# Input projection: late modulation blocks beside the first units, and twenty units as ten pairs of seven half-size products

## The chip, the cores and the metric

The kernel runs on one core of one Trainium2 chip. The metric is device time in microseconds (us) from start to end of one execution. The core has a matrix engine (TensorE, "PE" in rows), a vector engine (VectorE, "DVE"), a scalar engine (ScalarE, "ACT"), GpSimd ("POOL") and SyncE ("SP"), which here only issues DMAs. Each engine works through its own instructions in order and waits on semaphores that the others raise.

## The reference

One layer of a decoder trunk over T = 1088 tokens (1024 of a prompt, 64 of samples). What matters here is its first half:

```
mod = silu(c) @ w_ada + b_ada                    # c: 9 rows, w_ada: 1024 x 6144
h = rmsnorm(x, g_mix) * (1 + sc1) + sh1          # 1088 x 1024
z = h @ w_in                                     # columns: u, q, k, v, o, ig, fg, gp, gm
d = window means of u - u                        # pooling mixer
q, k, v, ig, fg -> mLSTM in chunks of 128 tokens
```

Everything is float32.

## The kernel before

**A split matmul.** TensorE multiplies rounded fp32r operands. For float32 accuracy each operand is split: ScalarE copies it rounded ("hi"), VectorE subtracts that from the original ("lo"), and TensorE sums three products, hi x hi, hi x lo and lo x hi. The activations h lie split in `act_hi` and `act_lo` (128 partitions, 8 blocks of 128 inputs each, 1088 tokens).

**A unit** is 128 output columns of a weight matrix over all 1088 tokens: its 512 KB of weights are loaded into `raw` (two slots), split into `w_hi` and `w_lo` by `split_hi` (L1028) and `split_lo` (L1588), and multiplied in 8 blocks x 3 products x 3 column groups (384, 384, 320) = 72 matmuls of L2340 into three PSUM banks of `dense` (two sets, turn by turn). `evac` (L1124, L1126) copies the sums to `stage`, and a DMA stores them in the DRAM scratch `z`.

**The input projection's first part** (`l1_part`) is 28 units after the gate unit, in z's order: u (4 units), q, k, v (8 each). The first runs together with the gate unit, so 27 stand in the stretch that changes. The mLSTM's second part (`U_L2` on) needs q, k and v back from z: `qk_load` and `v_load` wait until the stores have landed.

**Late modulation blocks.** 14 blocks of 256 columns of `w_ada` aren't needed until the second part. One goes with every two units: SyncE loads 1 MB into `ada_w`, ScalarE and VectorE split it (`wa_hi`, `wa_lo`), TensorE multiplies it with `c_hl` (16 matmuls, L2460 and L2461), ScalarE copies the result to `ada_rows`, TensorE turns it (L2471), and VectorE adds it to `mod` (L1706, L1709).

**Gate tables.** From ig and fg come small tables for the mLSTM; they are written to DRAM and read back in other layouts by SyncE (L605 to L621), in its one queue with all weight loads. TensorE turns the tables and the pooling history `hrow` (L2526) after the unit at which they are due. GpSimd computes the pooling mixer (L936 to L948), behind the history.

**The feed-forward part** has the scheme that the change brings to the input projection: seven products of half-size blocks in place of eight (Winograd's form of Strassen's scheme), with weight sums on VectorE (L2058 to L2065), splits of 512 columns (L1334, L2047), products of 24 matmuls of 272 columns (L2760), and partial sums taken by ScalarE (L1382 to L1394) and added by VectorE (L2100 to L2112). It runs two such chains side by side, turn by turn.

## Time and profile before

| | |
|---|---|
| median of 3 runs (lowest to highest) | 1964.58 us (1964.14 to 1965.5) |
| the profiled execution's own time | 1967.0 us |
| its span, first to last instruction | 1965.3 us |
| mean granted TensorE clock | 0.989 of full speed |
| busy: PE, DVE, ACT, POOL | 1908.4, 829.4, 621.2, 128.4 us |

The profile is of one execution. "Busy" counts an engine's own instructions, not its waits. In rows of a timeline the bracket at the end is the idle time just before, and what ended it; a row of the timeline that ends in x3 or x16 is several equal instructions in a row.

### The profile page before, as it was taken

How to read it: one execution, taken by the hardware profiler on the slowest of the kernel's cores; microseconds unless marked ns; L12 is line 12 of the kernel's file. 1: busy time of each engine (PE TensorE's matmuls, PEld its weight loads, DVE VectorE, ACT ScalarE, POOL GpSimd, SP SyncE). 2: the span in 40 equal slices, each digit the busy share in tenths (PEclk: the TensorE clock that was granted, in tenths of full speed). 3: DMA queues.
4: the chain of work that ended last, by engine and by line, in shares of the span. 5: the costliest groups of instructions: out<-in, count | busy, mean ns of one | idle time of the engine just before them, and what ended most of it. 6: DMA issues, size and time to landing. Idle time of an engine off the chain costs nothing.

```text
span 1965.3 us, 30471 instructions
## 1 busy us (share of the span) xinstructions
PE 1908.4 (97%) x12193; PEld 1815.0 (92%) x12193; DVE 829.4 (42%) x1363; ACT 621.2 (32%) x952; POOL 128.4 (7%) x245
## 2 busy tenths in 40 slices
PE   7999999999999999999999997899999999999998
PEld 4799989999999997777899997899999999999998
DVE  5422222213334333232553558844455545564542
ACT  4331222222434433121210215533333334343432
POOL 0010009201000002221000000000000000000000
PEclk9999999999999999999999998999999999999999
DMA  8653434452343345544642350422232223774641
GB/s 273 239 177 120 132 122 135 140 151 73 93 128 106 92 150 129 165 142 143 203 123 89 90 175 25 109 67 67 71 111 80 65 65 119 261 240 149 214 152 63
DMA packets 254045, 257.70 MB, mean 131 GB/s; under 512 B 15476, under 2 KB 213160, under 8 KB 253952
## 3 DMA queue, kind: packets, MB, share of 16 engines
q1 hardware_dynamic: 244830, 222.81, 37.7%
q10 hardware_dynamic: 7721, 29.25, 3.7%
q0 software_dynamic: 1408, 4.46, 0.8%
q8 instruction: 58, 0.95, 0.2%
q14 instruction: 28, 0.22, 0.0%
HBM read 189.97 MB, written 66.63 MB: 131 GB/s over the span
## 4 chain that ended last, share of the span: by engine, by line
PE 92%; DVE 3%; ACT 2%; DMA 1%; issue 1%; SPq 0%; ACTq 0%; DVEq 0%
PE dense L2340 44%; PE dense L2760 17%; PE dense L2805 10%; PE misc L2760 5%; PE misc L2805 3%; PE misc L2641 2%; PE misc L2628 1%; PE misc L2567 1%; PE misc L2571 1%; PE misc L2540 1%; DMA ada_w<-in_w_ada_dram 1%; PE dense L2414 1%; PE misc L2569 1%; PE misc L2461 1%; PE misc L2460 1%
## 5 line engine op out<-in xcount | busy, mean ns | idle before, releaser
L2340 PE MATMUL dense<-act_hi,w_hi 128*128 128x384 f32 x1704 | 401.2, 343 | 5.8 <-DVE act_lo L1593 3.0
L2340 PE MATMUL dense<-act_lo,w_hi 128*128 128x384 f32 x1704 | 377.4, 329 | 0.0
L2340 PE MATMUL dense<-act_hi,w_lo 128*128 128x384 f32 x1704 | 376.9, 329 | 0.0
L2340 PEld LDWEIGHTS dense<-act_hi,w_hi 128*128 128x128 f32 x1704 | 291.9, 189 | 28.3 <-issue 21.4
L2340 PEld LDWEIGHTS dense<-act_hi,w_lo 128*128 128x128 f32 x1704 | 293.0, 189 | 0.0
L2340 PEld LDWEIGHTS dense<-act_lo,w_hi 128*128 128x128 f32 x1704 | 292.0, 189 | 0.0
L1588 DVE TENSOR_TENSOR w_lo<-raw,w_hi 128x1024 fp32r<-128x1024 f32 x73 | 92.4, 1267 | 265.9 <-ACT w_hi L1028 265.8
L1124 ACT ACTIVATE stage<-dense 128x768 f32<-128x768 f32 x52 | 42.2, 812 | 285.1 <-PE dense L2340 285.0
L1028 ACT ACTIVATE w_hi<-raw 128x1024 fp32r<-128x1024 f32 x73 | 77.3, 1060 | 167.7 <-PE dense L2340 167.3
L2047 DVE TENSOR_TENSOR w_lo<-hmT,w_hi 128x512 fp32r<-128x512 f32 x120 | 78.9, 686 | 101.2 <-ACT w_hi L1334 101.2
L1334 ACT ACTIVATE w_hi<-hmT 128x512 fp32r<-128x512 f32 x120 | 72.6, 623 | 81.2 <-PE dense L2760 80.8
L2760 PE MATMUL dense<-act_hi,w_hi 128*128 128x272 f32 x528 | 89.0, 291 | 7.0 <-DVE sums L2100 5.6
L2760 PE MATMUL dense<-first_ops,w_hi 128*128 128x272 f32 x528 | 89.1, 291 | 4.2 <-DVE first_ops L2074 4.2
L2760 PE MATMUL dense<-act_lo,w_hi 128*128 128x272 f32 x528 | 87.7, 288 | 1.8 <-DVE w_lo L2047 1.8
L2760 PEld LDWEIGHTS dense<-act_hi,w_hi 128*128 128x128 f32 x528 | 75.7, 191 | 7.9 <-issue 7.0
L2760 PEld LDWEIGHTS dense<-first_ops,w_hi 128*128 128x128 f32 x528 | 75.4, 191 | 4.7 <-DVE first_ops L2074 2.8
L2760 PEld LDWEIGHTS dense<-act_lo,w_hi 128*128 128x128 f32 x528 | 74.7, 188 | 2.2 <-DVE w_lo L2047 2.2
L2228 DVE TENSOR_TENSOR w_lo<-raw,w_hi 128x1024 fp32r<-128x1024 f32 x34 | 41.6, 1224 | 60.1 <-ACT w_hi L1472 60.0
L2228 DVE TENSOR_TENSOR wx_lo<-stage,wx_hi 128x1024 fp32r<-128x1024 f32 x32 | 39.1, 1225 | 58.1 <-ACT wx_hi L1472 58.0
L2760 PE MATMUL dense<-last_op,w_hi 128*128 128x272 f32 x352 | 59.4, 292 | 2.9 <-issue 2.9
L1472 ACT ACTIVATE w_hi<-raw 128x1024 fp32r<-128x1024 f32 x34 | 36.0, 1059 | 75.2 <-PE misc L2805 37.0
L1472 ACT ACTIVATE wx_hi<-stage 128x1024 fp32r<-128x1024 f32 x32 | 33.8, 1059 | 71.5 <-PE misc L2805 40.2
(435 smaller groups left out, 3051.2 us busy)
## 6 DMA issues: line engine op xcount, KB each, us to landing
z_scratch<-stage ACTq DMA_DIRECT2D x52, 544.0 KB, 2.7
raw<-in_w_in_dram SPq DMA_DIRECT2D x53, 512.0 KB, 3.8
ada_w<-in_w_ada_dram SPq DMA_DIRECT2D x24, 1024.0 KB, 5.5
hmT<-in_w_gate_up_dram SPq DMA_DIRECT2D x40, 512.0 KB, 6.1
raw<-in_w_down_dram SPq DMA_DIRECT2D x34, 512.0 KB, 4.4
stage<-in_w_down_dram SPq DMA_DIRECT2D x32, 512.0 KB, 4.4
stage<-z_scratch SPq DMA_DIRECT2D x24, 544.0 KB, 3.7
a_scratch<-sums SPq DMA_DIRECT2D x34, 272.0 KB, 4.8
```

Of the source, the lines that this page charges most:

```text
L1028: act.activation(w_hi[:, n % 2, :], raw[:, n % 2, :], ACT.Copy).then_inc(hi_ready, 1)
L1124: act.activation(wide(stage[:, k % 2, :]), tile_wide(k), func)
L1334: act.activation(w_ops(d, st, q)[0], w_src(d, st, q), ACT.Copy).then_inc(whi_ready, 1)
L1472: act.activation(down_ops(v)[0], down_raw(v), ACT.Copy).then_inc(downhi_ready, 1)
L1588: dve.tensor_tensor(w_lo[:, n % 2, :], raw[:, n % 2, :], w_hi[:, n % 2, :].bitcast(F32), ALU.subtract).then_inc(raw_free[n % 2], 1)
L2047: dve.tensor_tensor(lo, w_src(d, st, q), hi.bitcast(F32), ALU.subtract).then_inc(wlo_ready, 1)
L2228: dve.tensor_tensor(lo, down_raw(v), hi.bitcast(F32), ALU.subtract).then_inc(downlo_ready, 1)
L2340: ins = pe.matmul(tile(k, c), w[:, n % 2, off:off + P], x[:, xr, t0:t1], start=(first and p == 0), stop=(last and p == 2))
L2414: ins = pe.matmul(ada_bank(e), cT[:, kk, :], w[:, kk, :], start=(kk == 0), stop=(kk == KT - 1))
L2641: give(pe.matmul(bank(r, E1), kb[:, b, P * a:P * a + P], vs[:, :], start=True, stop=True), r)
L2760: ins = pe.matmul(out[:, c, :], w[:, P * kt:P * kt + P], x[:, kt, HB * c:HB * c + HB], start=(st in FRESH and kt == 0 and p == 0), stop=(k ...
L2805: ins = pe.matmul(down_bank(ph, o, n), w[p // 2][:, 512 * f + P * o:512 * f + P * o + P], a[p % 2][:, f, 0:n], start=(u == 0 and f == 0 an ...
```

## The change

`l1_part` is gone. Units 1 to 7 after the gate unit's partner run one by one, each with two late modulation blocks between its eight blocks of inputs (`between`): half a block's product after input blocks 1 and 2, its turn after 4; the next one's halves after 5 and 6, its turn after 7. Splits of modulation blocks are done in halves too, and `ada_w` has two slots. The other 20 units become ten pairs: 256 columns over 1088 tokens as seven products of a half-size weight block (512 inputs x 128 columns) and a half-size activation block (512 inputs x 544 tokens). Four sums of activation blocks are made once, by GpSimd from `act_hi` and `act_lo` (ten operations of 2176 columns into `t32`), and split by `t_high` and `t_low`. The pooling mixer on GpSimd starts after all late modulation blocks. Pairs split their weights into halves of slot 0 of `w_hi` and `w_lo`; odd pairs are loaded into slot 1's place (`raw_a`, `raw_b`), even ones into `raw`.

```diff
-U_L1, U_L2, U_GM, U_BP, U_BM, U_OUT, U_FFN = 1, 29, 45, 53, 57, 65, 73
-T_SS, T_GATE, T_L1, T_L2, T_YP, T_BP, T_BM, T_OUT = 0, 1, 2, 30, 54, 58, 66, 74
+U_L1, U_L2, U_GM, U_BP, U_BM, U_OUT, U_FFN = 1, 9, 25, 33, 37, 45, 53
+T_SS, T_GATE, T_L1, T_L2, T_YP, T_BP, T_BM, T_OUT = 0, 1, 2, 10, 34, 38, 46, 54
...
+PAIRS, PAIR_ROW, PAIR_LOOPS = 10, 8, 4
+W0, WS0, G0, GU0 = STEPS * PAIRS, 4 * PAIRS, PAIRS, 16 * PAIRS
...
+        T_OPS = ((t12[:, 0], t12[:, 1]), (t12[:, 2], t12[:, 3]), (t34[:, 0], t34[:, 2]), (t34[:, 1], t34[:, 3]))
+        IN_OPS = (act_block(0, 0), act_block(1, 0), T_OPS[1], T_OPS[0], T_OPS[2], act_block(1, 1), T_OPS[3])
...
+            a, b = pair_raw(p)
+            return (a[:, 0:KB], a[:, KB:2 * KB], a[:, 0:KB], s1b, b[:, 0:KB], a[:, KB:2 * KB], b[:, KB:2 * KB])[st]
...
+            slot, r = (1, st) if p == 0 and st < 2 else (0, (STEPS * p + st) % 2)
+            return w_hi[:, slot, KB * r:KB * r + KB], w_lo[:, slot, KB * r:KB * r + KB]
...
+        def pair_banks(p, st):
+            if st % 2 == 0:
+                return bank_pair(0 if p % 2 == 0 else 3)
+            return bank_pair(1 if st == 1 else 2)
...
+            def late_ada_load(b):
+                if b >= 2:
+                    sp.wait_ge(ada_cut, 2 * (b - 1))
...
+            def pair_load(p, i=0):
+                for u in range(2):
+                    src = w_cols(w_in[0], i * (4 * P) + P * (PAIR_ROW + 2 * p + u))
+                    if u == 0:
+                        if p == 0:
+                            sp.wait_ge(raw_free[1], 4)
+                            sp.wait_ge(raw_free[0], 5)
+                        elif p == 1:
+                            sp.wait_ge(p_done, 2)
+                        else:
+                            sp.wait_ge(wlo_ready, at(p, STEPS, -STEPS, i))
+                    sp.dma_start(pair_raw(p)[u].rearrange("p (k n) -> p k n", k=KT), src).then_inc(gu_in[p % 2], 16)
+            load(4, w_cols(w_in[0], 3 * P))
+            for j in range(1, 5):
+                late_ada_load(2 * j)
+                load(j + 4, w_cols(w_in[0], P * (j + 3)))
+                late_ada_load(2 * j + 1)
+            for b in (10, 11):
+                late_ada_load(b)
...
-            l1_loads(4, 6)
-            load(28, w_cols(w_in[0], 27 * P))
+            for b in (12, 13):
+                late_ada_load(b)
+            pair_load(0)
+            pair_load(1)
+            with sp.Fori(0, PAIR_LOOPS) as i:
+                pair_load(2, i)
+                pair_load(3, i)
...
+            sp.wait_ge(wlo_ready, STEPS * (PAIRS - 1))
+            for j in range(2):
+                l2_load(j)
+            halves_out(6)
+            sp.wait_ge(p_done, STEPS * (PAIRS - 1) + 4)
             for c in range(2):
                 qk_load(c, c)
...
+            t1, t2_, t3, t4 = (t32[:, n] for n in range(4))
+            t_sum(t1, half_of(act_hi, 0, 1), half_of(act_hi, 0, 0))
+            t_sum(t2_, half_of(act_lo, 0, 1), half_of(act_lo, 0, 0))
+            t_done(t1, t1, t2_, ALU.add)
...
+            pool.wait_ge(ada_cut, 2 * ADA_LATE)
+            wait_full(pool, round_full, R_HROW)
...
+            def ada_high(b, half):
+                wait_full(act, ada_in, b, inc=16)
+                if b and half:
+                    wait_full(act, round_full, R_LATE["prod", b - 1])
+                elif b:
+                    act.wait_ge(half_prod, EP0 + b)
+                k0 = KH * half
+                act.activation(wa_hi[:, k0:k0 + KH, :], ada_w[:, b % 2, k0:k0 + KH, :], ACT.Copy).then_inc(adahi_ready, 1)
...
+            def prod_high(p, st, i=0):
+                if st == 0:
+                    act.wait_ge(gu_in[p % 2], i * 32 + 32 * (p // 2 + 1))
+                if st in (2, 3, 4, 5):
+                    act.wait_ge(wsum_ready, at(p, 4, {2: 3, 3: 1, 4: 2, 5: 4}[st], i))
+                if p or st > 3:
+                    act.wait_ge(p_done, at(p, STEPS, st - 1, i))
+                elif st < 2:
+                    wait_full(act, tile_full, T_L1 + 6)
+                else:
+                    wait_full(act, tile_full, T_L1 + 7)
+                act.activation(pair_ops(p, st)[0], pair_src(p, st), ACT.Copy).then_inc(whi_ready, 1)
...
+            def pair_take(p, st, n, sem_, i=0):
+                u, h = ((0, 0), (0, 1), (1, 1), (1, 0))[n]
+                act.wait_ge(p_done, at(p, STEPS, st + 1, i))
+                act.wait_ge(half_out[n], at(p, 16, HALF0[n], i))
+                act.activation(two(half_row(u, h)), pair_banks(p, st), ACT.Copy).then_inc(sem_, 1)
+            def pair_store(p, n, sem_, base=0, i=0):
+                u, h = ((0, 0), (0, 1), (1, 1), (1, 0))[n]
...
+                act.wait_ge(sem_, at(p, 1, base + 1, i))
+                act.dma_start(dst, half_row(u, h)).then_inc(half_out[n], 16)
+            def act_pair(p, i=0, last=False):
+                prod_high(p, 2, i)
+                pair_take(p, 0, 0, s1_ready, i)
+                prod_high(p, 3, i)
+                pair_store(p, 0, g1_ready, 0, i)
+                prod_high(p, 4, i)
+                pair_take(p, 2, 1, s2_ready, i)
+                prod_high(p, 5, i)
+                pair_take(p, 3, 2, s5_ready, i)
+                prod_high(p, 6, i)
+                if not last:
+                    prod_high(p + 1, 0, i)
+                pair_store(p, 2, u2_ready, 0, i)
+                if not last:
+                    prod_high(p + 1, 1, i)
+                else:
+                    act.wait_ge(wlo_ready, STEPS * PAIRS)
+                    split_hi(U_L2)
+                pair_take(p, 6, 3, u1_ready, i)
+                pair_store(p, 1, g2_ready, 0, i)
+                pair_store(p, 3, u1_ready, U1_0, i)
+                if last:
+                    split_hi(U_L2 + 1)
+            for j in range(1, 8):
+                k = T_L1 + j - 1
+                evac(k, 0)
+                evac(k, 1)
+                if j < 7:
+                    split_hi(U_L1 + j + 1)
+                store(k, z[j - 1])
...
+                for half in range(2):
+                    ada_high(2 * j - 1, half)
+                ada_copy(2 * j - 2)
...
+                if j < 7:
+                    for half in range(2):
+                        ada_high(2 * j, half)
+                if j == 5:
+                    t_high(0)
+                if j == 6:
+                    act.wait_ge(t_ready, T_0 + 1)
+                    act.wait_ge(t32_ready, T32_0 + 2)
+                    t_high(2)
+                if j == 7:
+                    for st in range(2):
+                        prod_high(0, st)
+                ada_copy(2 * j - 1)
...
+            def pair_low(p, st, i=0):
+                dve.wait_ge(whi_ready, at(p, STEPS, st + 1, i))
+                hi, lo = pair_ops(p, st)
+                dve.tensor_tensor(lo, pair_src(p, st), hi.bitcast(F32), ALU.subtract).then_inc(wlo_ready, 1)
+            def pair_sums(p, i=0):
+                a, b = pair_raw(p)
+                a11, a21, a22 = a[:, 0:KB], b[:, 0:KB], b[:, KB:2 * KB]
+                dve.wait_ge(wlo_ready, at(p, STEPS, 1, i))
+                dve.tensor_tensor(s1b, a21, a22, ALU.add).then_inc(wsum_ready, 1)
+                dve.wait_ge(wsum_ready, at(p, 4, 1, i))
+                dve.tensor_tensor(a21, a11, a21, ALU.subtract).then_inc(wsum_ready, 1)
+                dve.wait_ge(wsum_ready, at(p, 4, 2, i))
+                dve.tensor_tensor(a11, s1b, a11, ALU.subtract).then_inc(wsum_ready, 1)
+            def pair_last_sum(p, i=0):
+                a, _ = pair_raw(p)
+                dve.wait_ge(wsum_ready, at(p, 4, 3, i))
+                dve.wait_ge(wlo_ready, at(p, STEPS, 2, i))
+                dve.tensor_tensor(a[:, KB:2 * KB], a[:, KB:2 * KB], a[:, 0:KB], ALU.subtract).then_inc(wsum_ready, 1)
...
+                dst = two(half_row(u, h))
+                dve.tensor_tensor(dst, pair_banks(p, st), dst, ALU.add).then_inc(sem_, 1)
+            def dve_pair(p, i=0, last=False):
+                if p:
+                    pair_low(p, 1, i)
+                    pair_sums(p, i)
+                    pair_last_sum(p, i)
+                pair_low(p, 2, i)
+                pair_low(p, 3, i)
+                pair_add(p, 1, 0, s1_ready, g1_ready, i)
+                pair_low(p, 4, i)
+                if p == 0:
+                    t_low(3, 4)
+                pair_low(p, 5, i)
+                pair_low(p, 6, i)
+                pair_add(p, 4, 2, s5_ready, u2_ready, i)
+                if not last:
+                    pair_low(p + 1, 0, i)
+                pair_add(p, 5, 1, s2_ready, g2_ready, i)
...
+            def ada_product(b, half):
+                r = R_LATE["prod", b]
+                pe.wait_ge(ada_cut, 2 * b + half + 1)
+                if half == 0:
+                    take(r)
...
+            pe.wait_ge(c_ready, 1)
+            for j in range(1, 8):
+                def between(kk, j=j):
+                    if kk in (1, 2):
+                        ada_product(2 * j - 2, kk - 1)
+                    if kk == 3 and j == 3:
+                        gate_ends()
+                    if kk == 3 and j == 4:
+                        chunk_starts()
+                    if kk == 4:
+                        ada_turn(2 * j - 2)
+                    if kk in (5, 6):
+                        ada_product(2 * j - 1, kk - 5)
+                    if kk == 7 and j == 2:
+                        history_rows()
+                    if kk == 7 and j == 5:
+                        table_columns()
+                    if kk == 7:
+                        ada_turn(2 * j - 1)
+                unit(U_L1 + j, T_L1 + j, between=between)
...
+            def pair_product(p, st, i=0):
+                pe.wait_ge(wlo_ready, at(p, STEPS, st + 1, i))
+                if st == 0:
+                    if p == 0:
+                        wait_full(pe, tile_free, T_L1 + 6)
+                    elif p == 1:
+                        for r in (R_L2 - 2, R_L2 - 1):
+                            wait_full(pe, round_free, r)
+                    else:
+                        pe.wait_ge(u1_ready, at(p, 1, U1_0 - 1, i))
+                elif st in (1, 3):
+                    if p == 0:
+                        wait_full(pe, tile_free, T_L1 + 7)
+                    else:
+                        pe.wait_ge((g1_ready, g2_ready)[st // 2], at(p, 1, 0, i))
+                else:
+                    pe.wait_ge({2: s1_ready, 4: s2_ready, 5: s5_ready, 6: u2_ready}[st], at(p, 1, 1, i))
+                if p == 0 and st in (2, 3, 4, 6):
+                    pe.wait_ge(t_ready, T_0 + {2: 3, 3: 3, 4: 3, 6: 4}[st])
+                (w1, w2), (x1, x2) = pair_ops(p, st), IN_OPS[st]
+                out = pair_banks(p, st)
+                new = st in (0, 1, 3)
+                for kt in range(KH):
+                    for n in range(3):
+                        w, x = ((w1, x1), (w1, x2), (w2, x1))[n]
+                        for c in range(2):
+                            ins = pe.matmul(out[:, c, :], w[:, P * kt:P * kt + P], x[:, kt, HB * c:HB * c + HB],
+                                            start=(new and kt == 0 and n == 0),
+                                            stop=(kt == KH - 1 and n == 2), skip_group_check=not new)
+                ins.then_inc(p_done, 1)
...
+            pe.wait_ge(u1_ready, U1_0 + PAIRS - 1)
```

**SyncE, the loads around the table DMAs.** Names are destination and source. In the kernel before, the loop of unit and modulation loads ends, the tables follow, and the loop goes on:

```order
L540 DMA raw<-in_w_in_dram 128x8x128
L549 ISA
L549 DMA ada_w<-in_w_ada_dram 128x8x256
L596 REGISTER_ALU
L596 COMPARE_AND_BRANCH
L605 DMA negg_rows<-tab_negg 32x128
```

```order
L603 DMA ada_w<-in_w_ada_dram 128x8x256 x2
L595 DMA raw<-in_w_in_dram 128x8x128
L603 DMA ada_w<-in_w_ada_dram 128x8x256 x3
L671 DMA negg_rows<-tab_negg 32x128
L673 DMA tab_s<-tab_r 32x8
...
L681 DMA dec<-decay_rows 128x64
L683 DMA negg_s<-tab_s 64x256
L687 DMA scol<-tab_s 64x1 x16
L603 DMA ada_w<-in_w_ada_dram 128x8x256 x2
L660 DMA raw<-in_w_in_dram 128x8x128 x2
```

The second fence is the changed kernel: blocks 12 and 13 and the first pair's weights now stand behind all table DMAs, and no unit's weights are left there.

**ScalarE, after the fifth of the seven units.** First the kernel before, one unit of its loop, then the changed kernel from the split of block 9 to the copy of block 11 (`t<-t` is `t_high`):

```order
L1124 ACTIVATE stage<-dense 128x768
L1126 ACTIVATE stage<-dense 128x320
L1028 ACTIVATE w_hi<-raw 128x1024
L1130 DMA z_scratch<-stage 128x1088
L1147 ACTIVATE ada_rows<-misc 18x256
L1033 ACTIVATE wa_hi<-ada_w 128x2048
```

```order
L1143 ACTIVATE wa_hi<-ada_w 128x1024 x2
L1248 ACTIVATE ada_rows<-misc 18x256
L1143 ACTIVATE wa_hi<-ada_w 128x1024 x2
L1253 ACTIVATE t<-t 128x2176
L1248 ACTIVATE ada_rows<-misc 18x256
L1236 ACTIVATE stage<-dense 128x768
L1238 ACTIVATE stage<-dense 128x320
L1133 ACTIVATE w_hi<-raw 128x1024
L1242 DMA z_scratch<-stage 128x1088
L1143 ACTIVATE wa_hi<-ada_w 128x1024 x2
L1248 ACTIVATE ada_rows<-misc 18x256
L1143 ACTIVATE wa_hi<-ada_w 128x1024 x2
```

Before, the copy to `ada_rows` came ahead of the next block's split; now it comes behind that split, and twice behind `t_high` too.

**VectorE, one odd pair** of the changed kernel, from its second weight split on (the kernel before has one `w_lo<-raw,w_hi 128x1024` for each unit here):

```order
L1949 TENSOR_TENSOR w_lo<-raw_a,w_hi 128x512
L1956 TENSOR_TENSOR rows2k<-raw_b 128x512
L1958 TENSOR_TENSOR raw_b<-raw_a,raw_b 128x512
L1960 TENSOR_TENSOR raw_a<-rows2k,raw_a 128x512
L1967 TENSOR_TENSOR raw_a<-raw_a 128x512
L1949 TENSOR_TENSOR w_lo<-raw_a,w_hi 128x512
L1949 TENSOR_TENSOR w_lo<-rows2k,w_hi 128x512
L1975 TENSOR_TENSOR stage<-dense,stage 128x544
L1949 TENSOR_TENSOR w_lo<-raw_b,w_hi 128x512
```

The four weight sums stand between the splits for the pair's products 1 and 2 (counted from 0).

## Rows read from the trace of the kernel before

**Rows 1.** The page: the chain that ended last, shares of the span by engine.
```profile
PE 92%; DVE 3%; ACT 2%; DMA 1%; issue 1%; SPq 0%; ACTq 0%; DVEq 0%
```
**Rows 2.** Chain in order of time: start, length, what.
```profile
92.66 11.99 PE dense L2340 x72
...
441.09 12.01 PE dense L2340 x72
```
**Rows 3.** Window that changes: us; busy PE, PEld, DVE, ACT, POOL; clock, DMA, GB/s.
```profile
90.62:453.23 362.61, 358.58 (x2212) 349.00 (x2209) 82.27 (x115) 89.28 (x120) 69.74 (x63) 1.00 0.44 137
```
**Rows 4.** Timeline of PE: block product, unit, turn, next unit.
```profile
90.62 0.28 PE L2460 MATMUL misc<-wa_hi,c_hl 128*18 128x256 f32 x1
...
92.50 0.66 PE L2340 MATMUL dense<-act_hi,w_hi 128*128 128x384 f32 x3
...
...
104.58 0.29 PE L2471 MATMUL misc<-ident,ada_rows 18*128 18x18 f32 x2
104.81 0.78 PE L2340 MATMUL dense<-act_hi,w_hi 128*128 128x384 f32 x3
```
**Rows 5.** Timeline, windows (clock is the third last) and chain around the tables' turn.
```profile
293.59 0.63 PE L2526 MATMUL misc<-ident,hrow 120*128 120x120 f32 x4 [4.03 <-DVEq L1712]
...
295.00:297.00 2.00, 2.00 (x9) 2.00 (x8) 0.00 (x0) 0.00 (x0) 1.92 (x1) 0.50 0.07 21
...
294.22 13.53 PE dense L2340 x72
```
**Rows 6.** Chain, feed-forward part in its steady state.
```profile
1335.69 20.95 PE dense L2760 x168
```
**Rows 7.** Groups by form, ACT and DVE, 1290 to 1670 us.
```profile
L1334 ACT ACTIVATE w_hi<-hmT 128x512 fp32r<-128x512 f32 x109 | 66.1, 623 | 73.4 <-PE dense L2760 73.4
L1382 ACT ACTIVATE sums<-dense 128x544 f32<-128x544 f32 x10 | 6.3, 627 | 21.0 <-PE dense L2760 21.0
L2047 DVE TENSOR_TENSOR w_lo<-hmT,w_hi 128x512 fp32r<-128x512 f32 x109 | 71.8, 686 | 91.3 <-ACT w_hi L1334 91.3
L2058 DVE TENSOR_TENSOR rows2k<-hmT 128x512 f32<-128x512 f32 x18 | 12.4, 692 | 0.6
L2112 DVE TENSOR_TENSOR sums<-dense,sums 128x544 f32<-128x544 f32 x18 | 13.0, 724 | 23.6 <-PE dense L2760 23.6
```
**Rows 8.** Timeline of SyncE's queue: the table DMAs and the next unit load.
```profile
282.44 0.41 SPq L605 DMA_DIRECT2D negg_rows<-tab_negg  x1
...
304.59 7.61 SPq L540 DMA_DIRECT2D raw<-in_w_in_dram  x2
```
**Rows 9.** Instructions on tile ada_w, 85 to 460 us: ns min/median/max; then landing.
```profile
L1681 DVE TENSOR_TENSOR wa_lo<-ada_w,wa_hi x14: 2283/2292/4000, 84.8 to 417.1; 128x2048 fp32r<-128x2048 f32 x14
...
L1033 ACT ACTIVATE wa_hi<-ada_w x13: 1897/1899/1903, 93.1 to 415.2; 128x2048 fp32r<-128x2048 f32 x13
...
DMA to landing us min/median/max: 5.2/5.3/7.6
```
**Rows 10.** Timeline: GpSimd's pooling beside VectorE's splits.
```profile
309.98 1.66 DVE L1588 TENSOR_TENSOR w_lo<-raw,w_hi 128x1024 fp32r<-128x1024 f32 x1 [15.07 <-ACT w_hi L1028]
...
336.20 3.75 DVE L1588 TENSOR_TENSOR w_lo<-raw,w_hi 128x1024 fp32r<-128x1024 f32 x1 [9.78 <-ACT w_hi L1028]
336.94 1.93 POOL L936 TENSOR_TENSOR win<-ext_p 128x1038 f32<-128x1038 f32 x1
338.94 9.15 POOL L936 TENSOR_TENSOR win<-win 128x1036 f32<-128x1036 f32 x3
```
**Rows 11.** Chain and timeline at the start of the second part.
```profile
454.29 2.67 DMA z_scratch<-stage
...
461.22 0.93 PE L2540 MATMUL misc<-ident,qkv 128*128 128x128 f32 x4 [2.08 <-DMA qkv<-z_scratch]
```
**Rows 12.** Timeline of ACT: a unit's copies and splits after PE's last matmul.
```profile
439.24 0.81 ACT L1124 ACTIVATE stage<-dense 128x768 f32<-128x768 f32 x1 [10.35 <-PE dense L2340]
...
441.21 0.36 ACT L1147 ACTIVATE ada_rows<-misc 18x256 f32<-18x256 f32 x1
```

553 lines of the change are left out of this document (313 added, 240 removed).

## The prediction

> **What bounds the kernel now.** I read the chain that ended last first: TensorE is 92% of it [rows 1], so time is gained only where TensorE does less or waits less. In order of time the chain is one unit after another, each about 12.0 us, from the first of the 27 to the last [rows 2]. The window from the first late block's product at 90.62 us to the second part's first unit at 453.23 us is the stretch that changes: 362.6 us, with VectorE busy 82 us, ScalarE 89 us and GpSimd 70 us in it [rows 3]. The other engines have room; what can hurt is their order, not their load.
>
> The timeline gives the parts: a block's product (16 matmuls) is 92.50 - 90.62 = 1.88 us; unit and turn together end at 104.81, and the next unit's first group takes 0.78 us where another takes 0.66, so a turn costs 12.31 + 0.12 - 12.0 = 0.43 us [rows 4]. Once TensorE stands for 4.03 us (the turn of the history behind VectorE's additions), and afterwards the granted clock is 0.50, the lower level of 1.2 GHz, and the unit takes 13.53 us, 1.5 us more [rows 5]. Check: 27 x 12.0 + 14 x 1.88 + 14 x 0.43 + (4.0 + 1.5 + 0.7, the wait, its clock, and about 0.7 for the turns of tables and history) = 362.5 us, against 362.6 us.
>
> **The products.** The pair isn't in this trace as such, but the feed-forward part runs the same 24 matmuls of 272 columns per product: 168 of them, seven products, in 20.95 us, without a gap [rows 6]. That is 2.99 us a product, and one pair in 20.95 us against 2 x 12.0. Ten pairs: 240.0 - 209.5 = 30.5 us less. The 14 blocks' products and turns keep their number; halving a product adds no instruction. The 4.0 + 1.5 us of [rows 5] are gone, since tables and history are turned in different units and their bank is free by then; against that I count 0.5 us for turns that now stand singly. Without a new wait the stretch is 7 x 12.0 + 26.3 + 6.0 + 1.2 + 209.5 = 327.0 us, 35.6 us less.
>
> A page of the Trainium skill would size this otherwise: "TensorE: Matmul & The Clock Gate", section "Back-to-back issue gap", puts a warm matmul of N columns at N/2.4 + 2.5 ns. By that a pair is 168 x 115.8 ns = 19.5 us and two units 22.1 us, ten pairs gain 26.6 us, and the forecast would be 3.9 us later. The trace disagrees: 1088 columns take 500 ns as three matmuls (12.0 us / 24) and 499 ns as four (20.95 us / 42).
>
> **Does a pair hide its preparation?** The feed-forward part runs two chains side by side; here is one, so a weight half may be split only from the end of the product before last: 2.99 us instead of twice that. ScalarE 0.62 us, VectorE 0.69 us [rows 7], and about 0.25 us for three hand-overs (0.14 us from TensorE's end to ScalarE's start at 439.24 in [rows 12] is one of them): 1.6 us, slack 1.4 us. The tightest places: before product 2, VectorE does split, four sums, split, 0.7 + 4 x 0.69 + 0.69 = 4.1 us, from 0.75 us after product 0's start, so it ends at 4.9 of 6.0 us, slack 1.1 us. Before product 6 it does split and addition, 0.75 + 0.69 + 0.72 = 2.2 us, slack 0.8 us. ScalarE's takes are 0.63 us [rows 7], one per product at most beside a split. So alone no wait in pairs 1 to 9. In the first pair the split of an activation sum stands in the row as well (2.29 us for 2048 columns [rows 9], 2.4 us for 2176): 1.1 + 3 x 0.69 + 2.4 + 2 x 0.69 = 7.1 us against 6.0, a wait of 1.1 us, and 0.1 later: 1.2 us.
>
> **New waits in the units.** TensorE's turn of a block waits for ScalarE's copy to `ada_rows`. For the odd blocks TensorE has 1.5 us of matmuls in between (one input block of eight). ScalarE must first split the next block's second half, which waits for the same product: 0.14 + 0.95 + 0.3 + 0.1 = 1.5 us (half of 1.90 [rows 9], the copy's 0.36 [rows 12] overlapping): just hidden. In the fifth unit `t_high` stands ahead of the copy, 1.90 x 2176/2048 = 2.0 us: TensorE waits about 1.7 us there.
>
> In the sixth, block 12 must have landed first. A unit's period is 12.0 + 3.76 + 0.86 = 16.6 us, so unit 5 starts at 90.6 + 4 x 16.6 + 0.9 = 157.9. Block 11's load is issued once block 9's second half is split: 157.9 + 6.4 + 2.4 = 166.8. Then come the table DMAs. Before they took from 282.44 to the next load at 304.59, 22.1 us [rows 8], mostly issue time and a round trip to DRAM, which nothing here shortens. So block 12 is issued at 189.3, lands 5.3 us later [rows 9] at 194.7; two half splits 2.0, `t_high` 2.0, copy and hand-over 0.5: 199.2. TensorE arrives at the turn at 192.7. It waits 6.5 us, and I add the 1.5 us that the clock cost after the 4.03 us wait. Together 8.0 us. This takes the place of the wait removed. Block 13 and the first pair's weights are issued right behind and land by about 201, before they are due. A shorter path would need a shorter table sequence: the lower end is 2 us (only `t_high`), the upper 11 us if block 12 takes the longest landing, 7.6 us.
>
> **GpSimd beside VectorE.** In this stretch are two blocks of GpSimd work: ten sums of 2176 columns, 1.93 x 2176/1038 = 4.0 us each, 40 us beside units 1 to 5 (VectorE has about 7 us of work in 16.6 there, two block splits of 2.29 and the rest small), and the pooling mixer, which moves from units to the pairs. Beside pooling, VectorE's split of 1024 columns took 1.66 us once and 3.75 us once, and three GpSimd operations of 1.9 us took 9.15 us [rows 10]; the median of the 14 block splits is 2.29 us, the least 2.28, the longest 4.00 [rows 9]. The pooling is at most 70 us [rows 3], so four or five pairs have it beside them. Lower end: nothing (slack 1.1 and 1.4 us). Upper end: each such pair's 4.1 us sequence grows as 1.22 to 3.75, by 8.5 us, less 1.1 of slack, in four pairs 30 us. The rows lie nearer to 1.66, that is +35%: 4.1 us grow by 1.4 us, 0.3 us over the slack, and product 6's by 0.5, hidden. I take 0.7 us a pair, 3 us in all.
>
> **The end.** The second part's first V values are late by 2.08 us now [rows 11]: the last store is issued 1.2 us after the last unit, lands 2.67 us later. After the change the last half is copied (0.63) and stored behind one more store issue, 1.1 to 1.6 us after the last product. Same; 0.
>
> **Sum.** -35.6 + 8.0 + 1.7 + 1.2 + 3.0 = -21.7 us. Against the profiled execution's 1967.0 us, which lies 2.4 us over the median, that is 1945.3; against the median of 1964.58 it is 1943 us.
>
> **Rivals.**
> A, the forecast, 1943 us, its own range 1938 to 1949: 0.52.
> B, GpSimd costs more. If it goes first whenever both want the memory, VectorE loses in four or five pairs not 35% but nearly GpSimd's share: some 15 us more, 1958 us. For it speaks the 3.75 us row, against it the 1.66 us one. 0.15. The Trainium skill's page "GPSIMD Engine Reference", section "Specifications", says that GpSimd shares its SBUF interfaces with VectorE and contends with VectorE instructions that have two SBUF inputs, as all splits and weight sums have; by that rule B's mechanism is real, and the page gives no size.
> C, block 12 isn't waited for, since the round trip in the table DMAs (part of the 22.1 us) is shorter at another time or landing doesn't matter: 6 us less, 1937 us, 0.12.
> D, more waits in units 1 to 7, for instance each odd turn late by 1 to 2 us because the chain of 1.5 us is just hidden, or block loads late at 2 MB a unit: 7 x 1.4 = 10 us, 1953 us, 0.16.
> E, slower: the single chain of weight halves doesn't fit in a product. The place is the pair's split sequence; it decides from 21.7/70 = 0.31 us on each product, so if splits and hand-overs need 3.3 us instead of 1.6. Then 1965 and above, say 1972 at 3.4 us. Against it stand all rows of [rows 7]; only lasting contention would do it. 0.05.
>
> **How the numbers follow.** A measurement of this kernel can tell about 0.2%, 3.9 us, from no change. A to D are all beyond that on the faster side, E is slower, with 0.02 for a result between. The range from 1935 to 1957 takes in A, C, D and most of what lies between A and B, and leaves out E and B's end, some 0.2.
>
> **What the changed profile would show.** Products of 24 matmuls in 3.0 us, pairs in 21.0 us from the fifth on; one wait of TensorE of 6 to 7 us at the sixth unit's last turn, released by the copy, with block 12's landing ahead of it and a clock of 0.5 behind it; 1.7 us at the fifth's; about 1 us before the first pair's product 2; small waits before products 2 of pairs that have pooling beside them. The second part unchanged, with its 2 us wait for V. Wrong it goes if the pairs' products are spaced wider than 3.0 us, if TensorE waits at every unit, or if the tables' DMAs take another time.

## The result

The changed kernel is slower: 1988.39 us, median of 4 runs (1986.56 to 1988.89), against 1965.04 us (1964.14 to 1966.01, 4 runs) before; ratio 1.0116, 95% interval 1.0099 to 1.0132. The prediction of 1943 us was wrong in sign and by 45 us.

### The profile after

The profiled execution's span is 1986.7 us. First the chain of work that ended last, from the input projection's second half to its end (start, length, what); then PE's waits from 85 to 500 us (us in total, times, longest); then windows of the changed stretch, which name the busy time of PE, PEld, DVE, ACT and POOL (with the number of instructions) and then the granted clock, the DMA share and GB/s.

```profile
345.77 21.08 PE dense L2837 x168
...
451.17 3.03 PE misc L2837 x24
...
472.95 5.95 DMA z_scratch<-stage
...
478.97 4.18 DMA qkv<-z_scratch
```
```profile
PE misc L2732 <- DVE wa_lo L1874: 10.6, 4, 5.6
PE misc L2746 <- ACT ada_rows L1248: 9.0, 2, 7.4
PE dense L2837 <- DVE w_lo L1949: 6.9, 4, 2.6
PE misc L2865 <- DMA qkv<-z_scratch: 5.4, 1, 5.4
PE misc L2837 <- DVE w_lo L1949: 3.2, 3, 2.6
PE misc L2732 <- DVE ext_s L2013: 2.9, 1, 2.9
PE dense L2611 <- issue: 2.4, 1, 2.4
PE misc L2837 <- DVE stage L1975: 1.3, 1, 1.3
```
```profile
90.62:107.00 16.38, 14.90 (x87) 14.04 (x88) 15.24 (x4) 4.44 (x6) 16.14 (x4) 0.90 0.58 163
107.00:124.00 17.00, 13.22 (x77) 11.57 (x76) 16.64 (x12) 9.25 (x14) 16.84 (x4) 0.90 0.36 121
124.00:141.00 17.00, 10.22 (x54) 8.53 (x53) 16.80 (x8) 2.20 (x3) 16.77 (x4) 0.80 0.27 84
...
210.00:230.00 20.00, 12.65 (x67) 11.84 (x66) 5.90 (x11) 5.18 (x6) 0.00 (x0) 0.74 0.58 187
...
330.00:472.00 142.00, 142.00 (x1135) 142.00 (x1134) 62.41 (x92) 43.47 (x73) 2.35 (x4) 1.00 0.33 105
```

Three things are to be seen. The pairs do what was forecast: seven products in 21.08 us, no gap, full clock, from 330 us on. The loss lies before that. The stretch from the end of the two-unit part (89.7 us) to the last product (472.3) takes 382.6 us, where before it took 362.6 [rows 3]. And in the first three windows VectorE is busy nearly all the time (15 to 17 of 17 us) with four to twelve instructions, where the prediction had counted 7 us of work in a unit.

The timeline of VectorE and of GpSimd in units 1 to 3 shows why (start, length; x2 is two instructions):

```profile
87.78 10.06 DVE L1780 TENSOR_TENSOR w_lo<-raw,w_hi 128x1024 fp32r<-128x1024 f32 x2 [1.66 <-ACT w_hi L1133]
98.98 10.55 DVE L1874 TENSOR_TENSOR wa_lo<-ada_w,wa_hi 128x1024 fp32r<-128x1024 f32 x2 [1.14 <-ACT wa_hi L1143]
109.46 0.35 DVE L1892 TENSOR_SCALAR mod<-misc,vec 128x9 f32<-128x9 f32 x2
...
121.89 5.18 DVE L1780 TENSOR_TENSOR w_lo<-raw,w_hi 128x1024 fp32r<-128x1024 f32 x1 [0.15 <-DVE mod L1896]
...
139.30 4.18 DVE L1903 SCALAR_TENSOR_TENSOR tab_lf<-tab_fg,tab_ln 32x136 f32<-32x136 f32 x1 [0.16 <-DVE mod L1896]
...
148.48 1.23 DVE L1780 TENSOR_TENSOR w_lo<-raw,w_hi 128x1024 fp32r<-128x1024 f32 x1
150.99 1.22 DVE L1874 TENSOR_TENSOR wa_lo<-ada_w,wa_hi 128x1024 fp32r<-128x1024 f32 x1 [1.29 <-ACT wa_hi L1143]
```
```profile
86.01 4.91 POOL L995 TENSOR_TENSOR t<-act_hi 128x2176 f32<-128x2176 f32 x1
90.99 5.76 POOL L995 TENSOR_TENSOR t<-act_lo 128x2176 f32<-128x2176 f32 x1
...
108.53 5.69 POOL L998 TENSOR_TENSOR t<-t,act_lo 128x2176 f32<-128x2176 f32 x1
...
137.59 5.74 POOL L998 TENSOR_TENSOR t<-t,act_lo 128x2176 f32<-128x2176 f32 x1
```

While GpSimd makes its ten sums (86.0 to 143.3 us, 5.7 us each and not the 4.0 us of the prediction), a VectorE split of 1024 columns takes 5 to 5.8 us on the average of a row; behind them, at 150.99, it takes 1.22. Size doesn't matter: an operation of 32 x 136 took 4.18 us at 139.30. But two operations that read PSUM (`misc`) took 0.35 us together at 109.46, while a sum was under way. Each delayed operation looks like one that does nothing until the GpSimd instruction under way is about to end, and then takes its own time: the rows of two splits from 98.98 and 110.22 end at 109.53 and 121.19, 1.1 us behind the ends of two sums (108.46 and 120.10). Beside the pooling's sums it is the same at a smaller size:

```profile
274.43 3.02 DVE L1967 TENSOR_TENSOR raw_a<-raw_a 128x512 f32<-128x512 f32 x1
277.37 2.40 DVE L1949 TENSOR_TENSOR w_lo<-raw_a,w_hi 128x512 fp32r<-128x512 f32 x1
279.69 2.39 DVE L1949 TENSOR_TENSOR w_lo<-rows2k,w_hi 128x512 fp32r<-128x512 f32 x1
282.01 0.71 DVE L1975 TENSOR_TENSOR stage<-dense,stage 128x544 f32<-128x544 f32 x1
...
302.52 1.40 DVE L1958 TENSOR_TENSOR raw<-raw 128x512 f32<-128x512 f32 x1
303.95 0.69 DVE L1960 TENSOR_TENSOR raw<-rows2k,raw 128x512 f32<-128x512 f32 x1
```
```profile
274.96 1.92 POOL L1041 TENSOR_TENSOR win<-ext_p 128x1038 f32<-128x1038 f32 x1
276.97 4.57 POOL L1041 TENSOR_TENSOR win<-win 128x1036 f32<-128x1036 f32 x2
...
302.01 3.07 POOL L1050 TENSOR_SCALAR win<-win 128x1008 f32<-128x1008 f32 x1
```

GpSimd's instructions end at 276.88 and 281.54, and VectorE's three, 0.69 us each elsewhere [rows 7], end at 277.45, 279.77 and 282.08: the first and the last half a microsecond behind them. The fourth, with a PSUM input, is not longer. The last row of GpSimd is the exception to keep in mind: this operation with one SBUF input takes 3.07 us, and VectorE's operation at 302.52 ends at 303.92, 1.2 us before it, and the next at 303.95 isn't delayed at all. So the pooling's one-input operation holds VectorE up at its start only, in no kept trace by more than 0.9 us.

The row at 274.43 has a further twist: VectorE's operation starts at 274.43, half a microsecond ahead of GpSimd's at 274.96, and yet ends behind it; so does the 3.75 us row of the kernel before (336.20 against 336.94 [rows 10]). What decides who goes first when both start so close together isn't shown.

TensorE's waits, in order: 2.42 us at 92.10 (the view names only "issue", but the first of the two `w_lo` splits from 87.78 ends just there), four for `wa_lo` (2.06, 1.72, 5.57, 1.21), one for `ext_s` (2.86), so 15.8 us in units 1 to 3; 1.61 and 7.35 us for ScalarE's copy at 198.56 and 223.96; eight in the first pairs, 11.4 us. Sum 36.2 us, where before there were 4.0 [rows 5]. At the end V's first product waits 5.4 us instead of 2.1 [rows 11]. In the windows with waits the granted clock is below 1.00; 90 to 330 us has a mean of 0.91, where before had 0.99:

```profile
90.00:330.00 240.00, 203.97 (x1318) 189.89 (x1319) 157.16 (x165) 80.11 (x114) 120.37 (x67) 0.91 0.44 138
```

(1.00 - 0.91) x 240 = 22 us. I use the two columns, waits and 240 us times what the clock lacks, as a rough account of each run below: it counts the clock during the waits too, where it costs nothing, and closes within 4 us.

### The profile page after: what moved, and what is told of

It reads as the page before. It is cut to its first block, busy times and chain, and to the rows that moved or that the text cites. A ratio compares the mean times of both kernels' runs of the same rounds, so it can differ in the third digit from the quotient of the medians.

```text
span 1986.7 us, 31328 instructions
## 1 busy us (share of the span) xinstructions
PE 1896.8 (95%) x12433; PEld 1798.5 (91%) x12433; DVE 967.2 (49%) x1501; ACT 655.4 (33%) x1020; POOL 186.7 (9%) x255
## 4 chain that ended last, share of the span: by engine, by line
PE 86%; DVE 7%; ACT 2%; DMA 2%; issue 2%; SPq 1%; ACTq 0%; DVEq 0%
PE dense L2611 29%; PE dense L3086 17%; PE dense L3131 10%; PE dense L2837 6%; PE misc L3086 5%; PE misc L3131 3%; PE misc L2837 3%; DVE wa_lo L1874 2%; PE misc L2967 2%; PE misc L2954 1%; PE misc L2893 1%; PE misc L2897 1%; PE misc L2865 1%; PE dense L2685 1%; PE misc L2895 1%
## 5 line engine op out<-in xcount | busy, mean ns | idle before, releaser
L2611 PE MATMUL dense<-act_hi,w_hi 128*128 128x384 f32 (+1 forms) x1224 | 297.8, 352 | 8.3 <-issue 3.3
L2611 PE MATMUL dense<-act_lo,w_hi 128*128 128x384 f32 (+1 forms) x1224 | 274.0, 332 | 0.0
L2611 PE MATMUL dense<-act_hi,w_lo 128*128 128x384 f32 (+1 forms) x1224 | 272.9, 331 | 0.0
L2611 PEld LDWEIGHTS dense<-act_hi,w_hi 128*128 128x128 f32 x1224 | 210.7, 191 | 31.8 <-issue 24.1
L2611 PEld LDWEIGHTS dense<-act_hi,w_lo 128*128 128x128 f32 x1224 | 212.9, 191 | 0.0
L2611 PEld LDWEIGHTS dense<-act_lo,w_hi 128*128 128x128 f32 x1224 | 212.5, 191 | 0.0
L1133 ACT ACTIVATE w_hi<-raw 128x1024 fp32r<-128x1024 f32 x53 | 56.0, 1058 | 168.9 <-PE dense L2611 166.3
L3086 PE MATMUL dense<-act_hi,w_hi 128*128 128x272 f32 x528 | 89.6, 293 | 6.0 <-DVE sums L2371 5.6
L3086 PEld LDWEIGHTS dense<-act_hi,w_hi 128*128 128x128 f32 x528 | 76.3, 192 | 6.7 <-issue 5.8
L1874 DVE TENSOR_TENSOR wa_lo<-ada_w,wa_hi 128x1024 fp32r<-128x1024 f32 x28 | 59.8, 2152 | 44.9 <-ACT wa_hi L1143 44.7
L3086 PEld LDWEIGHTS dense<-act_lo,w_hi 128*128 128x128 f32 x528 | 74.7, 188 | 2.2 <-DVE w_lo L2318 2.2
L2837 PE MATMUL dense<-t,w_hi 128*128 128x272 f32 x400 | 67.7, 292 | 4.7 <-DVE w_lo L1949 4.7
L3086 PE MATMUL dense<-last_op,w_hi 128*128 128x272 f32 x352 | 59.5, 292 | 2.9 <-issue 2.9
L2837 PEld LDWEIGHTS dense<-t,w_hi 128*128 128x128 f32 x400 | 57.5, 192 | 5.1 <-issue 2.8
```

The lines of the kernel that those rows point to most:

```text
L1133: act.activation(w_hi[:, n % 2, :], raw[:, n % 2, :], ACT.Copy).then_inc(hi_ready, 1)
L1874: dve.tensor_tensor(wa_lo[:, k0:k0 + KH, :], ada_w[:, b % 2, k0:k0 + KH, :], wa_hi[:, k0:k0 + KH, :].bitcast(F32), ALU.subtract).then_inc( ...
L2611: ins = pe.matmul(tile(k, c), w[:, n % 2, off:off + P], x[:, xr, t0:t1], start=(first and p == 0), stop=(last and p == 2))
L2837: ins = pe.matmul(out[:, c, :], w[:, P * kt:P * kt + P], x[:, kt, HB * c:HB * c + HB], start=(new and kt == 0 and n == 0), stop=(kt == KH ...
L3086: ins = pe.matmul(out[:, c, :], w[:, P * kt:P * kt + P], x[:, kt, HB * c:HB * c + HB], start=(st in FRESH and kt == 0 and p == 0), stop=(k ...
```

## The experiments

Theory G: GpSimd's instructions hold VectorE's up, the ten sums beside the units above all. Rivals: weight blocks or ScalarE's copies are late and VectorE only shows it; the pairs' own chain doesn't fit. Runs 3, 6 and 8 leave out a part of the output (the pooling's window sums, the activation sums, the window sums again), so they are bounds and no candidates. Ratios are against runs of the kernel before beside each set of experiments (medians 1965.0 to 1965.6 us). The last two columns show for each run PE's waits from the two-unit part to the last product and (behind the plus) the wait for V, and the mean clock from 90 to 330 us.

| run | edit | median us | ratio to before, 95% | PE waits us | clock |
|---|---|---|---|---|---|
| before | | 1965.0 | | 4.0 + 2.1 | 0.99 |
| changed | | 1988.39 | 1.0116 (1.0099 to 1.0132) | 36.2 + 5.4 | 0.91 |
| 1 | sums on VectorE | 1964.81 | 0.9993 (0.9985 to 1.0002) | 20.3 + 5.4 | 0.95 |
| 2 | blocks ahead of tables | 1984.73 | 1.0086 (1.0070 to 1.0103) | 33.3 + 5.4 | 0.92 |
| 3 | no pooling sums | 1969.94 | 1.0017 (1.0008 to 1.0026) | 26.0 + 5.5 | 0.94 |
| 4 | 1, 2 and copy first | 1940.40 | 0.9869 (0.9855 to 0.9884) | 6.2 + 5.4 | 1.00 |
| 5 | ten sums in pieces | 1967.91 | 1.0011 (1.0001 to 1.0021) | 22.0 + 5.6 | 0.95 |
| 6 | ten one-input operations | 1994.66 | 1.0152 (1.0135 to 1.0169) | 36.8 + 5.4 | 0.89 |
| 7 | 4, and V's loads earlier | 1936.15 | 0.9852 (0.9836 to 0.9869) | 5.6 + 1.5 | 1.00 |
| 8 | 7 without pooling sums | 1930.04 | 0.9821 (0.9804 to 0.9837) | 1.9 + 1.5 | 1.00 |
| 9 | 7, pooling in pieces | 1933.31 | 0.9835 (0.9822 to 0.9848) | 3.4 + 1.5 | 1.00 |
| 10 | before, with ten GpSimd operations | 1966.56 | 1.0007 (0.9998 to 1.0016) | 4.3 + 2.1 | 0.99 |

Steps between neighbouring runs of under some 4 us (2 against the changed kernel, 7 against 4, 9 against 7) lie where the intervals overlap. There the waits in the traces carry the reading, not the medians alone.

### 1: the ten sums on VectorE

```diff
-            t_sum(t1, half_of(act_hi, 0, 1), half_of(act_hi, 0, 0))
-            t_sum(t2_, half_of(act_lo, 0, 1), half_of(act_lo, 0, 0))
...
+            SUMS = [(t1, half_of(act_hi, 0, 1), half_of(act_hi, 0, 0), SUB, 0),
+                    (t2_, half_of(act_lo, 0, 1), half_of(act_lo, 0, 0), SUB, 0),
...
             for j in range(1, 8):
                 if j < 7:
                     split_lo(U_L1 + j + 1)
+                next_sum()
...
                 ada_add(2 * j - 2)
+                next_sum()
```

> The changed kernel with one edit: the ten activation sums that GpSimd computes beside units 1 to 5 are computed by VectorE, two in each unit; all else as in the changed kernel. Theory G (VectorE's splits with two SBUF inputs wait behind GpSimd's operations with two SBUF inputs): the two-split groups of units 1 to 3 fall from about 10 us to 2.4 us, the four waits of PE for w_lo and wa_lo and the one for ext_s (15.8 us in all) go, and with them the low clock of that stretch, 7 to 9 us: about 1965 us. Rival B (the weight blocks or ScalarE's copies come late, and VectorE only appears to be slow): the splits stay long and the time stays at 1985 to 1990 us. Rival R (VectorE has no room for ten more operations): new waits in the same units, 1975 us or more.

Measured 1964.81 us, 23.6 us less. In units 1 to 3 PE has no wait and the clock is 1.00; VectorE does the ten sums in 2.4 us each besides and has room for them, so R falls, and so does B: nothing was changed for loads or copies. By the two columns, 15.9 us are waits and 9.6 clock (0.04 x 240), 25.5 together. Alone this brings the kernel back to the time of before, not below.

### 2: modulation blocks ahead of the tables

```diff
-            for b in (10, 11):
+            for b in (10, 11, 12, 13):
                 late_ada_load(b)
+            pair_load(0)
...
-            for b in (12, 13):
-                late_ada_load(b)
-            pair_load(0)
             pair_load(1)
```

> The changed kernel with one edit: on SyncE's queue, the loads of modulation blocks 12 and 13 and of the first pair's weights stand ahead of the loads of the tables; the second pair's behind them. Theory Q (block 12 waits behind the tables' transfers): the wait of 7.35 us at unit 6's last turn goes, and with it most of the low clock behind it: 7 to 10 us less than the changed kernel, about 1980 us. Rival (what is late is ScalarE's or VectorE's share of block 12): the wait keeps more than 5 us, 1987 us. Second rival: the tables now come late for GpSimd's pooling or for the first pair, and a wait of some us appears there, 1984 us or more.

Measured 1984.73 us (six runs, one of them at 1974.63, the others 1983.3 to 1985.5), 3.7 us less than the changed kernel and half of what theory Q said; the two intervals overlap, so the median alone doesn't tell the step from none. The trace does: PE's two waits for `ada_rows` fell from 9.0 to 3.9 us, but the waits beside the pooling (for `w_lo`, and 1.3 us for `stage`) rose from 11.4 to 13.5 us:

```profile
PE dense L2835 <- DVE w_lo L1947: 8.0, 4, 4.6
PE misc L2835 <- DVE w_lo L1947: 5.5, 1, 5.5
...
PE misc L2744 <- ACT ada_rows L1246: 3.9, 2, 2.2
```

So Q has the mechanism, and 2.1 us of its 5.1 us went into waits beside the pooling, which meets the pairs at another moment (its first operation starts 5.5 us behind the first pair's first product, 4.0 us in the changed kernel). No new wait is for the tables, so the second rival falls.

### 3: without the pooling's sums

```diff
-                for smp_part in (False, True):
-                    n = HIST + (NT if smp_part else SEQ)
...
-                    link(pool.tensor_tensor(cut(ext, HIST, n), cut(dst, HIST, n), cut(ext, HIST, n), ALU.subtract))
                 pool.dma_start(z[Z_D + g, :, 0:SEQ], ext_p[:, g, HIST:HIST + SEQ]).then_inc(d_out, 16)
```

> The changed kernel with GpSimd's window sums of the pooling mixer left out (its loads and stores stay, so the pooling's part of the output is not computed). Theory G: VectorE's w_lo splits of 512 columns fall from 2.4 to 3.0 us back to 0.7 us, the eight waits for w_lo in the first three pairs (11.4 us) go, and 3 to 5 us of low clock: about 1973 us. Rival (the pairs' weights come late from the queue): the waits stay, 1986 us. By the price of the prediction, 3.0 us, it would be 1985 us.

Measured 1969.94 us, 18.4 us less. The `w_lo` splits are at 0.69 us again, PE's waits for them fall from 10.1 to 0.6 us and the one for `stage` goes. The first pair's product 2, which the prediction had waiting 1.1 us even so, waits 0.31:

```profile
249.81 0.77 PE L2813 MATMUL dense<-t,w_hi 128*128 128x272 f32 x4 [0.31 <-DVE w_lo L1925]
```

The pooling costs 18 us here, six times what the prediction gave it. The pairs' own chain fits when nothing stands beside it, so rival E's mechanism is out except for the contention that it named as its one condition.

### 4: three edits together

Experiments 1 and 2, and ScalarE's copy ahead of `t_high` in units 5 and 6:

```diff
+                if j < 7:
+                    ada_copy(2 * j - 1)
                 if j == 5:
                     t_high(0)
...
                 if j == 7:
                     for st in range(2):
                         prod_high(0, st)
-                ada_copy(2 * j - 1)
+                    ada_copy(2 * j - 1)
```

> The changed kernel with three edits: the ten activation sums on VectorE, the blocks 12 and 13 and the first pair's weights ahead of the tables on SyncE's queue, and ScalarE's copy of the modulation rows ahead of t_high in units 5 and 6. If the causes add, as theories G and Q say: less by 22 to 24 us for the sums, 8 us for the queue and 2 us for the copy: 1953 to 1957 us, which is below the kernel before. Rival (the waits overlap: PE's slack taken by one is needed by the next): 1960 to 1965 us, no better than the first experiment alone.

Measured 1940.40 us, 13 us below what was expected, and 1.3% faster than before. The account closes roughly: 30.0 us of waits and 0.09 x 240 = 21.6 of clock are 51.6, against 48.0 measured. What the expectation had not counted is that the waits beside the pooling fall too, from 11.4 to 4.9 us. In this run pooling's first operation stands at 214.79 us, 6.7 us behind the first pair's first product, when that pair's early splits are done; in the changed kernel it is 4.0 us behind (247.15 and 243.17), in experiment 1 4.5, in experiment 2 5.5, and these three have 11.4 to 13.5 us of such waits. That this phase is the reason is argued from the timelines, not shown by a run that moves only it. The copy's edit has no run of its own either; the 1.61 us wait that it aims at is gone.

### 5: each sum in four pieces

```diff
             def t_sum(dst, x, y, op=ALU.subtract):
-                link(pool.tensor_tensor(dst, x, y, op))
+                for k in range(KH):
+                    ins = pool.tensor_tensor(dst[:, k], x[:, k], y[:, k], op)
+                link(ins)
```

and the same in `t_done`.

> The changed kernel with one edit: each of GpSimd's ten activation sums is four operations of 544 columns instead of one of 2176. Work and place are the same. Theory W (a VectorE operation with two SBUF inputs waits until the GpSimd operation under way has ended): the 1024-column splits beside the sums fall from 5.2 us to 2.5 to 3 us, half to nine tenths of the 15.8 us of waits go, and the sums themselves take longer: 1966 to 1975 us. Theory S (the two engines share by rate, so that only the bytes count): the splits stay at 5 us and the time at 1985 to 1990 us.

Measured 1967.91 us: 20.5 of the 23.6 us of experiment 1 come back with all ten sums still on GpSimd. Same bytes, same engine, same place; only the instructions are shorter. That decides for W against S. From the timelines, three of VectorE's rows, and the four pieces of one sum beside the first:

```profile
107.71 1.61 DVE L1784 TENSOR_TENSOR w_lo<-raw,w_hi 128x1024 fp32r<-128x1024 f32 x1 [0.15 <-DVE mod L1900]
...
128.19 4.71 DVE L1878 TENSOR_TENSOR wa_lo<-ada_w,wa_hi 128x1024 fp32r<-128x1024 f32 x2
...
137.08 1.22 DVE L1927 COPY mprow<-mnext 1x28 f32<-1x28 f32 x1
```
```profile
106.00 8.20 POOL L996 TENSOR_TENSOR t<-act_hi,t 128x544 f32<-128x544 f32 x4
```

A split takes 1.3 to 2.4 us, a piece 1.4 us by itself and 2.2 to 2.4 us when a split comes in between (3.9 us with two of them). GpSimd pays: the ten sums take 73.4 us of busy time instead of 57, in part since its pieces wait for VectorE's instructions in turn. The last row shows more than theory W says: a copy with one SBUF input, 0.17 us in the changed kernel, took 1.22 us beside a piece. So two SBUF inputs aren't the only case that is held up.

### 6: one input instead of two

```diff
-                link(pool.tensor_tensor(dst, x, y, op))
+                link(pool.tensor_scalar(dst, x, 1.0, None, ALU.mult))
```

and the same in `t_done`.

> The changed kernel with the ten activation sums replaced on GpSimd by ten operations of the same 2176 columns with one input (a multiplication by one), so that the sums are not computed. Theory T (both engines must read two SBUF inputs to collide): the splits of units 1 to 3 are back at 1.2 us and the waits of 15.8 us go, 1963 to 1968 us, as with the sums on VectorE. Rival U (any GpSimd operation holds VectorE's two-input operations up): the splits stay at 3 to 5 us, and the time is 1975 us or more.

Measured 1994.66 us, slower than the changed kernel by 6 us. Theory T falls: these GpSimd operations with a single SBUF input hold VectorE up as well, and as they are longer (6.33 us) they do so for longer.

```profile
100.14 11.08 DVE L1874 TENSOR_TENSOR wa_lo<-ada_w,wa_hi 128x1024 fp32r<-128x1024 f32 x2 [1.75 <-ACT wa_hi L1143]
```
```profile
104.04 6.33 POOL L995 TENSOR_SCALAR t<-act_hi 128x2176 f32<-128x2176 f32 x1
```

Of VectorE's operations here, those with two SBUF inputs are long and those with a PSUM input are not. GpSimd's side isn't settled: the ten operations here hold VectorE up nearly to their end, the pooling's one-input operation of 1008 columns only at its start (302.01 above), and no run has a GpSimd operation that reads nothing from SBUF. What makes the difference stays open.

### 7: V's loads ahead of the second keys

```diff
-            for c in range(2):
-                qk_load(c, c)
+            qk_load(0, 0)
             halves_out(PAIRS)
-            for c in range(2):
-                v_load(c, c)
+            v_load(0, 0)
+            qk_load(1, 1)
+            v_load(1, 1)
```

> The kernel of the fourth experiment (1940.4 us) with one more edit: at the end of the input projection SyncE's queue carries the loads for the attention's first products in the order qk 0, v 0, qk 1, v 1 instead of qk 0, qk 1, v 0, v 1. Theory (PE's wait of 5.4 us ahead of V's first product is for a transfer behind 1 MB that nobody needs yet): the wait falls to 2 to 3 us and the time to 1936 to 1938 us. Rival (the wait is for the last store of the projection, which takes 6 us to land): no change, 1940 us.

Measured 1936.15 us, 4.3 us below experiment 4; V's wait is 1.5 us. Both sides had half of it: V's loads wait for the last store, as the rival said, but in experiment 4 that store took 6.16 us, with the loads for two of the attention's chunks issued ahead of it. With the second chunk's moved behind it, it lands in 2.10 us:

```profile
424.58 2.10 DMA z_scratch<-stage
```

### 8: nothing of GpSimd beside the projection

The diffs of experiments 7 and 3 together.

> The kernel of the seventh experiment with GpSimd's window sums of the pooling mixer left out too, so that GpSimd computes nothing beside the input projection (the pooling's part of the output is not computed). A bound on what the last overlap costs. Theory G: the remaining waits for w_lo in the pairs (4.9 us in the fourth experiment) and 2 us of clock go: 6 to 8 us below the seventh experiment, 1929 to 1932 us. Rival (only waits of the first pair's t and of the queue are left): within 3 us of the seventh experiment.

Measured 1930.04 us. PE waits 1.9 us from the two-unit part to the last product, the clock is 1.00, the last product ends at 420.15:

```profile
417.15 3.00 PE misc L2819 x24
```
```profile
90.00:330.00 240.00, 237.92 (x1732) 227.30 (x1731) 139.38 (x206) 96.35 (x142) 11.91 (x17) 1.00 0.51 157
```

From the two-unit part's end (a unit's last matmul, some 89.6 us) that is 330.5 us. The prediction's 327.0 without waits, plus 1.9 of waits and 10 x 0.13 (21.08 instead of 20.95 us a pair), is 330.2. Of the 58.4 us between this and the changed kernel, 34.3 + 3.9 are waits and some 20, the rest, I put to the clock.

### 9: pooling in pieces

```diff
+                    def parts(lo, hi):
+                        w = hi - lo if smp_part else -(-(hi - lo) // 4)
+                        return [(p, min(p + w, hi)) for p in range(lo, hi, w)]
...
-                        link(pool.tensor_tensor(cut(dst, 2 * span - 1, n), cut(src, 2 * span - 1, n),
-                                                cut(src, span - 1, n - span), ALU.add))
+                        for lo, hi in parts(2 * span - 1, n):
+                            ins = pool.tensor_tensor(cut(dst, lo, hi), cut(src, lo, hi),
+                                                     cut(src, lo - span, hi - span), ALU.add)
+                        link(ins)
```

and the same for the two operations that end each window.

> The kernel of the seventh experiment (1936.15 us) with one more edit: each of GpSimd's pooling operations over the 1024 prompt columns is four operations of a quarter of the columns. Theory W (VectorE waits for the GpSimd operation under way, not for GpSimd's bytes): the w_lo splits of 1.6 to 2.8 us in the first pairs fall to about 1 us, PE's 4.3 us of waits for w_lo to 1 or 2 us, and the time to 1932 to 1934 us; without GpSimd's sums at all it was 1930.04 us. Rival: four operations cost GpSimd so much more that pooling reaches into more pairs, or the head tables behind it come late: 1936 us or more.

Measured 1933.31 us, 1.65% faster than before, with the whole output computed. The median is 2.8 us below experiment 7's, half of the 6.1 us that the pooling still cost there, though the two intervals overlap; PE's waits fell from 5.6 to 3.4 us. The lines for the pairs, where 4.3 us became 2.1:

```profile
PE dense L2853 <- DVE w_lo L1936: 1.5, 3, 1.0
...
PE misc L2853 <- DVE w_lo L1936: 0.6, 1, 0.6
```

### 10: the same GpSimd load in the kernel before

```diff
             link(last)
+            pool.wait_ge(hlo_ready, KH)
+            flat = win[:, :, :].rearrange("p s t -> p (s t)")
+            for n in range(10):
+                link(pool.tensor_tensor(flat[:, 0:2076], act_hi[:, 0:4, :].rearrange("p k t -> p (k t)")[:, 0:2076].bitcast(F32),
+                                        act_hi[:, 4:8, :].rearrange("p k t -> p (k t)")[:, 0:2076].bitcast(F32), ALU.add))
             link(pool.memset(ext_p[:, :, 0:HIST], 0.0))
```

> The kernel before with ten GpSimd additions of 2076 columns (two SBUF inputs, their results used by nothing) beside its units 1 to 5, where the changed kernel has its ten sums; nothing else is changed. Theory W: each VectorE split under way in those 57 us lasts until the GpSimd operation has ended, 5 to 6 us instead of 1.2 or 2.3, ten or eleven of them; a unit of 12.0 us has three, which want 17 us, so that PE waits some us in three or four units and loses clock behind it: 10 to 25 us more than before, 1975 to 1990 us. Rival (the ten sums hurt only since the changed kernel has four such splits and more in a unit): no PE wait, within 2 us of before.

Measured 1966.56 us, no change that can be told; my forecast of 10 to 25 us fell, and the rival holds. The splits are delayed here too:

```profile
96.85 6.77 DVE L1686 TENSOR_TENSOR wa_lo<-ada_w,wa_hi 128x2048 fp32r<-128x2048 f32 x1
...
118.18 1.45 DVE L1593 TENSOR_TENSOR w_lo<-raw,w_hi 128x1024 fp32r<-128x1024 f32 x1 [7.88 <-ACT w_hi L1033]
120.23 6.10 DVE L1686 TENSOR_TENSOR wa_lo<-ada_w,wa_hi 128x2048 fp32r<-128x2048 f32 x1 [0.60 <-ACT wa_hi L1038]
```

but PE waits 0.3 us for them. By a VectorE turn I mean here one such operation together with the wait before it (not TensorE's turn of a block). From 99 to 141 us this kernel has three unit splits and one block split, so about four turns of at most 6.1 us in 42 us, and VectorE still idles 7.88 us before one. The changed kernel has five splits in each unit of 17 us (one of the unit, four halves of two blocks): 5 x 5.7 = 28 us. Its timeline agrees: from one unit's split to the next, 121.89 to 148.48, VectorE needed 26.6 us. In experiment 5 five turns of at most 2.4 us make 12 us, and PE waits 0.2 us in units 1 to 3 (and 1.8 us for ScalarE's copy at the end of unit 4). So what counts is how many turns VectorE needs in a unit, times the length of one turn, against the unit; three kernels agree with this sum, and it is no more than that.

The ten operations also show GpSimd's side. The sixth, which began with VectorE idle, took 4.67 us; those that began as a split of 1024 columns was still under way took 5.54 to 5.56 us, and the two behind a block split of 2048 columns 6.6 us:

```profile
113.87 4.67 POOL L917 TENSOR_TENSOR win<-act_hi 128x2076 f32<-128x2076 f32 x1
118.62 5.56 POOL L917 TENSOR_TENSOR win<-act_hi 128x2076 f32<-128x2076 f32 x1
```

So the 5.7 us of a sum in the changed kernel holds, by this comparison, about a microsecond in which GpSimd waited for VectorE. The engines alternate, an instruction each, and both get longer.

## Why the prediction was wrong

**The products, -35.6 us: right.** Pairs run in 21.08 us, and experiment 8 has the stretch within half a microsecond of the sum. Its 1930.04 us is the time the prediction would have had with no price on waits: 1964.58 - 35.6 = 1929.0. The 19.5 us a pair of the prediction came from the formula in the Trainium skill's page "TensorE: Matmul & The Clock Gate", section "Back-to-back issue gap". The page gives that formula for an isolated matmul and says itself that a stream of them is spaced otherwise, so the prediction used it where it doesn't apply; the trace has 21.08 us.

**GpSimd beside VectorE, +3.0 us: the step that failed.** It failed twice. The ten sums were listed, with their 40 us and their place, and given no price, because VectorE's load there was 7 of 16.6 us; I compared loads, when what counts is turns. They cost 15.8 us of waits and with their clock 23.6 us (experiment 1). Their length was too short as well: 4.0 us was scaled from the pooling's row of 1038 columns, and even the first sum, which began as VectorE's last split was ending, took 4.91 us. And the pooling was priced as a rate, +35%, from the 1.66 us row rather than the 3.75 us one [rows 10]; they are no two samples of one rate. The split of 3.75 us ended at 339.95, 1.1 us behind a GpSimd operation with two SBUF inputs (338.87). The one of 1.66 us (309.98 to 311.64) stood beside the pooling's one-input operation, 2.74 us from 309.53, and ended before it did:

```profile
309.53 2.74 POOL L945 TENSOR_SCALAR win<-win 128x1008 f32<-128x1008 f32 x1
```

The row that I took for the rule was the one beside the mild kind. The pooling cost 18.4 us (experiment 3). The 4.1 us chain before product 2 had 1.1 us of slack, and one wait of 2.4 us uses that up.

**Block 12 behind the tables, +8.0 us: right in place and nearly in size.** 7.35 us of wait at unit 6's last turn, released by ScalarE's copy, with a window clock of 0.74. The tables took 24.7 us (189.72 to 214.43), not 22.1. In experiment 2 its removal was worth 3.7 us, within the margin of the two medians: part is given back beside the pooling.

**`t_high` ahead of the copy, +1.7: right**, 1.61 us.

**First pair's product 2, +1.2: too high**, 0.31 us once the pooling is away.

**The end, 0: wrong by 3.3 us.** The store's landing was taken from the trace before, 2.67 us; after, the loads for two of the attention's chunks are issued ahead of it, and it lands 5.95 us after issue.

**Clock.** I had added 1.5 us for one wait. Sixteen waits of 0.2 to 7.4 us stand at short distances, and the mean clock of 240 us is 0.91: some 20 us, more than half of what the waits themselves cost. The split into waits and clock is an account by the columns above, not an experiment.

Sum: the prediction had 13.9 us of waits and clock on top of -35.6; the changed kernel has 36.2 + 3.3 + 20, which gives 1964.58 - 35.6 + 59.5 = 1988.5.

**Rivals.** B named the contention, but not its form: it had GpSimd going first and VectorE getting a share, where the traces show whole instructions taking turns. What the Trainium skill's page "GPSIMD Engine Reference", section "Specifications", says of it, contention with VectorE instructions that have two SBUF inputs, the trace bears out: 5.18 us for a split with two, 0.35 us for two operations that read PSUM. B also put it in the pairs only, at 1958 us and 0.15. A sentence that says a mechanism is real should have sent me to every place where both engines work, not to the one where I had a row. C didn't occur. D had a right place, more waits in units 1 to 7, and 10 us for them, but neither of its causes: TensorE's 15.8 us of waits in units 1 to 3 went with the ten sums (experiment 1), and no odd turn waited for its copy outside the two places named. E ended on the right side, but its chain fits by itself; only the lasting contention that it named as the way there was real, and for the first pairs only.

## What to carry to other kernels

Beside GpSimd, count VectorE's operations, not its load: each one with two SBUF inputs, however small, may last about as long as the GpSimd instruction beside it, so their number per period times that length must fit in the period. If they don't, cut GpSimd's instructions into pieces (20.5 us back for the sums) or give the work to VectorE if it has the time (23.6). Price several short waits with the clock behind them, and run the waits' repairs together: alone two of them gave 23.6 and 3.7 us, together with a third small one 48.0 (why the three give more than their sum is argued above, not shown).

## What the runs showed of the hardware

- A VectorE split of 1024 columns, 1.22 us alone, took 5 to 5.8 us (average of a row) beside GpSimd operations of 5.7 us, 5.5 to 6.5 us beside one-input ones of 6.33 us, and 1.3 to 2.4 us beside the same work in pieces of 1.4 to 2.4 us. A 32 x 136 operation took 4.18 us instead of 0.29. Operations that read PSUM kept their time (0.35 us for two of 128 x 9, 0.71 us for 128 x 544).
- The pooling's one-input operation on GpSimd (128 x 1008) delayed VectorE at its start only: a 512-column operation took 1.40 us at 302.52, the next 0.69 us, both ended before it.
- A VectorE copy of 1 x 28 with one SBUF input took 1.22 us instead of 0.17 beside a GpSimd piece (experiment 5).
- The waiting goes both ways: 2076 columns on GpSimd took 4.67 us alone and 5.56 us when a split was under way at its start (experiment 10). The pooling's first operation (128 x 1038), 1.93 us at 336.94 in the kernel before, took 3.16 us in the changed kernel, where a VectorE operation of 2.42 us had begun 1.0 us ahead of it.
- 2176 columns in four pieces took 6.3 to 8.9 us, against 4.9 to 5.9 in one instruction.
- A store of 128 x 544 landed in 2.10 us with the loads of one attention chunk issued ahead of it and in 5.95 to 6.53 us with those of two.
- A wait of 1.61 us at 198.56 had a window of 0.91 behind it (192 to 210 us) in the changed kernel, while one of 2.01 us in experiment 4 left its window (230 to 245 us) at 1.00. What decides between them these runs don't show.
